# Feed-forward up products by seven half-size products, and modulation sums moved to other stages

## The reference

```python
def conv_glu(h, w_up, conv_w, conv_b, w_down):
    gate, val = jnp.split(h @ w_up, 2, axis=-1)          # h 256x1024, w_up 1024x5632
    gate = causal_dwconv(gate, conv_w) + conv_b          # 3 taps along the tokens
    return (jax.nn.silu(gate) * val) @ w_down            # w_down 2816x1024
...
for i in range(DEPTH):
    ...
    x = x + conv_glu(rms_norm(x, norm_ffn_w[i]), ffn_w_up[i], ffn_conv_w[i], ffn_conv_b[i], ffn_w_down[i])
...
cond = jax.nn.silu(c)
mod = cond @ w_ada[l] + b_ada[l]                         # w_ada 1024x6144, one row of condition
```

## Time and profile before

| | us |
|---|---|
| median of 3 runs | 2525.71 |
| lowest and highest run | 2521.23, 2529.0 |
| the profiled execution | 2521.13 |
| its span | 2519.2 |

### The profile page before, as it was taken

The page is one execution under the profiler, slowest core; times in us unless marked ns, Lnnn a source line. Parts: engine busy times, 40 slices in busy tenths (PEclk is TensorE's granted clock), DMA queues, the critical chain, the costliest instruction groups (busy, mean ns, idle before and its releaser), DMA issues.

```text
span 2519.2 us, 29772 instructions
## 1 busy us (share of the span) xinstructions
PE 2257.0 (90%) x12084; PEld 1458.6 (58%) x12084; DVE 927.0 (37%) x2253; ACT 555.2 (22%) x1232; POOL 57.9 (2%) x86
## 2 busy tenths in 40 slices
PE   8999999999999999999998887788799988777875
PEld 7888768855875787467764333333468743333332
DVE  4764437431143556243433222222324342222223
ACT  4321411001152210031622111111214421111111
POOL 0010000000100000002000000000002000000000
PEclk9999999999999999999999999998899989999998
DMA  7221236774721767735248999999733459999996
GB/s 274 101 76 68 103 131 250 264 285 160 209 105 67 264 230 266 267 128 167 101 176 341 427 427 427 428 428 427 283 142 118 160 245 427 427 428 428 427 427 269
DMA packets 141890, 653.57 MB, mean 259 GB/s; under 512 B 7386, under 2 KB 13834, under 8 KB 117040
## 3 DMA queue, kind: packets, MB, share of 16 engines
q1 hardware_dynamic: 138336, 642.19, 64.3%
q0 software_dynamic: 3408, 9.38, 1.6%
HBM read 648.40 MB, written 3.15 MB: 259 GB/s over the span
## 4 chain that ended last, share of the span: by engine, by line
PE 65%; DMA 24%; DVE 6%; ACT 3%; issue 1%; DVEq 0%; ACTq 0%
PE ps L106 63%; DMA wring<-in_w_up 11%; DMA AR<-in_w_up 5%; DMA wring<-in_w_gate 5%; PE ps L109 2%; DMA bias_rows<-AR 2%; ACT AR L115 1%; DVE AR L125 1%; DMA AR<-in_w_gate 1%; DVE AR L129 1%; ACT L115 1%; DVE AR L120 1%; DVE AR L133 0%; DVE X L125 0%; DVE XN L133 0%
## 5 line engine op out<-in xcount | busy, mean ns | idle before, releaser
L106 PE MATMUL ps<-HT,wring 128*128 128x256 f32 x3200 | 720.5, 386 | 0.8 <-ACT wring L115 0.4
L106 PEld LDWEIGHTS ps<-HT,wring 128*128 128x128 f32 x3200 | 616.0, 194 | 92.5 <-issue 4.2
L106 PE MATMUL ps<-wring,AR 128*32 128x512 f32 (+3 forms) x1440 | 348.7, 597 | 22.4 <-DVE AR L125 21.1
L115 ACT ACTIVATE AR<-ps 128x512 f32<-128x512 f32 (+4 forms) x338 | 162.3, 480 | 900.0 <-PE ps L106 849.9
L106 PE MATMUL ps<-wring,MN 128*32 128x512 f32 (+1 forms) x1568 | 246.2, 649 | 91.1 <-DMA wring<-in_w_up 73.5
L106 PEld LDWEIGHTS ps<-wring,AR 128*32 128x32 f32 (+1 forms) x1440 | 133.9, 145 | 183.7 <-issue 178.9
L106 PEld LDWEIGHTS ps<-wring,MN 128*32 128x32 f32 (+1 forms) x1568 | 68.6, 122 | 257.7 <-DMA wring<-in_w_up 107.8
L141 DVE COPY AR<-ps 128x512 f32<-128x512 f32 (+4 forms) x99 | 58.8, 594 | 383.4 <-PE ps L106 380.9
L106 PE MATMUL ps<-AR 128*128 128x128 f32 (+5 forms) x1336 | 183.2, 380 | 10.5 <-DVE AR L125 8.1
L125 DVE TENSOR_TENSOR AR<-ps,AR 128x128 f32<-128x128 f32 (+3 forms) x148 | 63.1, 426 | 326.7 <-ACT AR L115 163.3
L106 PEld LDWEIGHTS ps<-AR 128*128 128x128 f32 (+3 forms) x1336 | 132.6, 173 | 41.2 <-issue 30.3
(11 more groups left out here) (152 smaller groups left out, 1667.6 us busy)
## 6 DMA issues: line engine op xcount, KB each, us to landing
wring<-in_w_up SPq DMA_DIRECT2D x46, 2048.0 KB, 31.0
wring<-in_w_down SPq DMA_DIRECT2D x46, 2048.0 KB, 31.7
wring<-in_w_gate SPq DMA_DIRECT2D x44, 2048.0 KB, 27.3
wring<-in_w_ada SPq DMA_DIRECT2D x24, 2048.0 KB, 12.8
wring<-in_ffn_w_up SPq DMA_DIRECT2D x20, 2048.0 KB, 8.3
AR<-in_w_gate SPq DMA_DIRECT2D x20, 2048.0 KB, 27.8
wring<-in_w_in SPq DMA_DIRECT2D x18, 2048.0 KB, 7.7
AR<-in_w_down SPq DMA_DIRECT2D x18, 2048.0 KB, 32.2
```

The lines of the kernel that those rows point to most:

```text
L106: return Ins(self.eng and self.eng.matmul(out, lhs, rhs, start=start, stop=stop), None)
L115: return Ins(self.eng and self.eng.activation(out, in_, func, **kw), self)
```

## The change

The product of a chunk's weights (two k-halves by two column halves, quarters a11, a12, a21, a22) with HT (two k-halves by two token halves, quarters b11 to b22) is made by Strassen's scheme in Winograd's form: seven products of quarters, each of four k-tiles against 128 tokens, instead of eight. VectorE forms four sums of token quarters once per layer (in XN, `TS`), and four sums of weight quarters per chunk: s1 into `SUMS`, s3, s2 and s4 in place in the weights. The products go in pairs to PA banks (p26, p57, p34) and the first to PB, from which ScalarE copies it (`KEPT`). VectorE combines them in `RAWS`, from where the taps and the multiplication read; the middle tap moves to ScalarE. The order of products on TensorE is 1, 2, 7, 5, 6, 3, 4; in the first two chunks products 1 and 2 come before the rest, those of chunk 0 even before token half 1 is turned. `up_sums` of chunks 0 and 1 stand on VectorE ahead of the output projection's additions.

The down loads now start with the one that needs value chunk 0, each group waits for its own value chunk, and a bank of PA is taken at its first use. The 24 modulations leave the up phase: eight go to `down` of each layer (one, two, two and three after the first four groups), eight to sparse attention (two after each of the first three chunks, one after each of the last two). SyncE's order of loads, TensorE's sums and VectorE's passes follow.

The core of the diff (lines left out are "..."):

```diff
+    SUMS = Ring([at(4096 + 1024 * j, 1024) for j in range(2)])
+    KEPT = Ring([at(6144 + 256 * j, 256) for j in range(2)])
+    RAWS = Ring([at(8752 - 1024 * j, 1024) for j in range(2)])
...
+    UPS = [(val, chunk) for val in range(2) for chunk in range(6)]
+    ADA_DOWN = [(0,), (1, 2), (3, 4), (5, 6, 7)]
+    ADA_NSA = [(8, 9), (10, 11), (12, 13), (14,), (15,)]
+    DOWNS = (1, 0, 2, 3, 4, 5)
...
+    def up_blocks(i):
+        return 2 if UPS[i][1] < 5 else 1
...
+        n = 128 * up_blocks(i)
+        wt = blocks(W[up_name(layer, i)], 8, 2 * n)
+        total = SUMS[up_name(layer, i)][:, 0:4 * n].rearrange("p (k n) -> p k n", k=4)
+        return wt[:, 0:4, 0:n], wt[:, 4:8, 0:n], wt[:, 0:4, n:2 * n], wt[:, 4:8, n:2 * n], total
...
-            for val in range(2):
-                for chunk in range(6):
-                    n = 512 if chunk < 5 else 256
-                    c0 = val * 2816 + chunk * 512
-                    weights(("up", layer, val, chunk), up[:, c0:c0 + n], 8, n)
-                    if chunk < 5:
-                        ada(12 * layer + 5 * val + chunk)
-            weights(("down", layer, 0), dn[2560:2816], 2, 1024)
-            ada(12 * layer + 10)
-            weights(("down", layer, 1), dn[0:512], 4, 1024)
-            ada(12 * layer + 11)
-            for c in range(1, 5):
-                weights(("down", layer, 1 + c), dn[c * 512:c * 512 + 512], 4, 1024)
+            for i, (val, chunk) in enumerate(UPS):
+                n = 256 * up_blocks(i)
+                c0 = val * 2816 + chunk * 512
+                weights(up_name(layer, i), up[:, c0:c0 + n], 8, n)
+            for g, j in enumerate(DOWNS):
+                c0, n = (512 * (j - 1), 4) if j else (2560, 2)
+                weights(("down", layer, j), dn[c0:c0 + 128 * n], n, 1024)
+                for a in ADA_DOWN[g] if g < 4 else ():
+                    ada(16 * layer + a)
...
+            for n in ADA_NSA[ch]:
+                ada(n)
...
-            for m in range(2):
-                for c in range(2):
-                    bank(e, PA, (tag, m, c))
...
+                        if n == 0:
+                            bank(e, PA, (tag, m, c))
...
+            def product(i, part):
+                name, nb = up_name(layer, i), up_blocks(i)
+                a11, a12, a21, a22, total = up_tiles(layer, i)
+                if part == 1:
+                    bank(e, PB, ("p1", name))
+                    place(name)
+                    lhs, rhs, to = a11, HT[:, 0:4, tok(0)], (PB["p1", name], 0)
+                    e.wait_ge(sig("norm_ha"), (tag, 0, 3))
+                elif part == 2:
+                    bank(e, PA, ("p26", name))
+                    lhs, rhs, to = a12, HT[:, 4:8, tok(0)], (PA["p26", name], 0)
+                    e.wait_ge(sig("norm_ha"), (tag, 0, 7))
+                elif part == 7:
+                    bank(e, PA, ("p57", name))
+                    lhs, rhs, to = a21, TS[2], (PA["p57", name], nb)
+                    e.wait_ge(vect, ("t", layer, 2))
+                    e.wait_ge(vect, ("s3", name))
+                elif part == 5:
+                    lhs, rhs, to = total, TS[0], (PA["p57", name], 0)
+                    e.wait_ge(vect, ("t", layer, 0))
+                    e.wait_ge(vect, ("s1", name))
+                elif part == 6:
+                    lhs, rhs, to = a11, TS[1], (PA["p26", name], nb)
+                    e.wait_ge(vect, ("t", layer, 1))
+                    e.wait_ge(vect, ("s2", name))
+                elif part == 3:
+                    bank(e, PA, ("p34", name))
+                    lhs, rhs, to = a12, HT[:, 4:8, tok(1)], (PA["p34", name], 0)
+                    e.wait_ge(sig("norm_ha"), (tag, 1, 7))
+                    e.wait_ge(vect, ("s4", name))
+                else:
+                    lhs, rhs, to = a22, TS[3], (PA["p34", name], nb)
+                    e.wait_ge(vect, ("t", layer, 3))
+                ps, b0 = to
+                for b in range(nb):
+                    for k in range(4):
+                        c = 128 * (b0 + b)
+                        ins = e.matmul(ps[:, c:c + 128], lhs[:, k, 128 * b:128 * b + 128], rhs[:, k, :], k == 0, k == 3)
+                ins.then_inc(done, (name, part))
+                if part == 4:
+                    W.free(name, (done, (name, 4)))
+                elif part == 5:
+                    SUMS.free(name, (done, (name, 5)))
+            product(0, 1)
+            product(0, 2)
             norm_half(tag, 1)
-            for val in range(2):
-                for chunk in range(6):
-                    n = 512 if chunk < 5 else 256
-                    name = ("up", layer, val, chunk)
-                    features(done, name, weights(name, 8, n), 8, HT, range(0, n, 128), tag)
-                    W.free(name, (done, (name, n // 256 - 1)))
-                    k = 12 * layer + 5 * val + chunk
-                    if chunk < 5 and k > 12 * layer:
-                        ada_sum(k - 1)
-            e.wait_ge(sig("ffn_v"), ("val", layer, 21))
-            srcs = [(("down", layer, 0), 20, 2)] + [(("down", layer, 1 + c), 4 * c, 4) for c in range(5)]
-            down(done, tag, srcs, G, [lambda n=n: ada_sum(12 * layer + 9 + n) for n in range(3)], None if layer else "nsa")
+            for i, part in ((1, 1), (1, 2), (0, 7), (0, 5), (0, 6), (0, 3), (0, 4), (1, 7), (1, 5), (1, 6)):
+                product(i, part)
+            PA.defer()
+            product(1, 3)
+            product(1, 4)
+            for i in range(2, 12):
+                for part in (1, 2, 7, 5, 6, 3, 4):
+                    product(i, part)
+            srcs = [(("down", layer, j), 4 * (j - 1) if j else 20, 4 if j else 2) for j in DOWNS]
+            ready = [(vect, ("val", layer, j - 1 if j else 5)) for j in DOWNS]
+            down(done, tag, srcs, G, [lambda ns=ns: [ada_sum(16 * layer + n) for n in ns] for ns in ADA_DOWN],
+                 None if layer else "nsa", ready)
...
+                for n in ADA_NSA[ch]:
+                    ada_sum(n)
...
+                for n in ADA_NSA[3 + ch]:
+                    ada_sum(n)
...
+            for i in range(2):
+                up_sums(layer, i)
...
+            a11, a12, a21, a22, total = up_tiles(layer, i)
+            v.wait_ge(slots[W.where[name]], name)
+            v.tensor_tensor(total, a21, a22, ADD).then_inc(done, ("s1", name))
+            v.tensor_tensor(a21, a11, a21, SUB).then_inc(done, ("s3", name))
...
+                v.wait_ge(mm, (name, part))
+                if part == 1:
+                    v.tensor_tensor(a11, total, a11, SUB).then_inc(done, ("s2", name))
+                else:
+                    v.tensor_tensor(a12, a12, a11, SUB).then_inc(done, ("s4", name))
...
+                v.wait_ge(act, ("p1", name))
+                v.wait_ge(mm, (name, 6))
+                v.tensor_tensor(r[:, :, :, 0, :], both(i, "p26"), two(p1), ADD).then_inc(done, ("u2", name))
+                KEPT.free(name, (done, ("u2", name)))
+                PA.free(("p26", name), (done, ("u2", name)))
+                v.tensor_tensor(r[:, :, :, 1, :], both(i, "p57"), two(r[:, 1, :, 0, :]), ADD).then_inc(done, ("u4", name))
...
+                v.wait_ge(mm, (name, 4))
+                v.tensor_tensor(crossed, both(i, "p34"), r[:, :, :, 1, :], ADD).then_inc(done, ("c21", name))
+                PA.free(("p34", name), (done, ("c21", name)))
+                v.tensor_tensor(r[:, 1, :, 1, :], both(i, "p57")[:, 0], r[:, 1, :, 1, :], ADD).then_inc(done, ("c22", name))
+                PA.free(("p57", name), (done, ("c22", name)))
...
+                if val:
+                    g = G[:, 4 * chunk:4 * chunk + n, :]
+                    v.wait_ge(act, ("gate", layer, 4 * chunk + n - 1))
+                    v.tensor_tensor(g, RAWS[name][:, 0:256 * n].rearrange("p (b t) -> p b t", b=n), g, MUL).then_inc(done, ("val", layer, chunk))
+                    RAWS.free(name, (done, ("val", layer, chunk)))
+                else:
+                    for b in range(n):
+                        f = 4 * chunk + b
+                        y, x = G[:, f, :], RAWS[name][:, 256 * b:256 * b + 256]
+                        v.wait_ge(act, ("center", layer, f))
+                        for d in (2, 1):
+                            ins = v.scalar_tensor_tensor(y[:, d:256], x[:, 0:256 - d], vec("fconv", 66 * layer + f + 22 * (2 - d)), y[:, d:256], MUL, ADD)
+                            ins.then_inc(done, ("gate", layer, f) if d == 1 else None)
+                    RAWS.free(name, (done, ("gate", layer, f)))
...
+            b11, b12, b21, b22 = (HT[:, 4 * k:4 * k + 4, tok(m)] for k in range(2) for m in range(2))
+            v.wait_ge(sig("norm_mm"), (tag, 1, 1))
+            v.wait_ge(sig("norm_ha"), (tag, 0, 7))
+            v.tensor_tensor(TS[0], b12, b11, SUB).then_inc(done, ("t", layer, 0))
+            v.wait_ge(sig("norm_ha"), (tag, 1, 7))
+            v.tensor_tensor(TS[2], b22, b12, SUB).then_inc(done, ("t", layer, 2))
```

(54 more changed lines are left out.)

71 lines of the change are left out of this document (42 added, 29 removed).

## The result

The kernel after takes **2562.61 us** (median of 4 runs, 2559.54 to 2564.69), the kernel before 2525.99 (4 runs of the same chip): ratio **1.0146**, 95% interval 1.0127 to 1.0165. The forecast had the sign and most of the mechanisms, and was 17.6 us too low; the upper end of its range was missed by 0.6 us.

What follows compares the result with a forecast made beforehand. TensorE, busy 90% of the span, was taken as the bound. Gains of -39.1 and costs of +58.9 gave +19.8 us on the profiled 2521.1, so 2540.9; with 4.6 for the median, 2545 us, range 2517 to 2562.

Steps and rivals of the forecast that it cites:

- A: Up phase, TensorE: seven products of 128 columns for eight in 256-column calls, 303.6 us becomes 275.0, -28.6 us.
- B: Start of both up phases: products 1 and 2 of chunk 0 fill TensorE's gaps, -6.5 us, and one clock drop goes, -1.7.
- C: Passage from up to down: the first down group wants only value chunk 0, so the wait goes, -2.3 us.
- D: VectorE in the up phase: late sum in chunk 5, +4.8 us; satisfied waits and nearly full VectorE, +5 (0 to 17).
- E: Moved modulations in the downs: third sum after group 3 waits for its VectorE pass, +4.2 and +5.9 us (0 to 15).
- F: Moved modulations in sparse attention: loads held up by the bias-row write, then VectorE late, +35 us (13 to 45).
- the landing of `n2` at T+48: Sparse attention: third projection chunk's weights land 48 us after the first projection (T, 604.46 us); TensorE stalls 15 us.
- by T+24.5 about half of n2 has come: Sparse attention, when the bias-row write's slow part begins: 275 packets of that weight load still lie on held engines.
- Clock drops after the new stalls, 1.7 each: Sparse attention: two or three drops of TensorE's clock behind the new stalls, +4 us.
- 1: Rival, sparse attention: weight packets are not held up, one PSUM bank is; 12.6 us instead of 35, 2521 us, chance 0.15.
- 3: Rival, up phase: the seven products are not cheap, 0.1 to 0.2 us lost at each of 168; 2560 to 2575, chance 0.05.
- 2: Rival, sparse attention: the bias-row write no longer reaches into the projections, nothing there waits; 2507 us, chance 0.10.

## Why the prediction was right, and where it was short

- **A** right. In after the records keep 0.112 us, and the product stage is worth what the sum said, within 3 us (experiment with the products of before).
- **B, C** right: both gaps at the start and the one at the passage are gone.
- **D** right for chunk 5 (2.79 us for 2.4, and 6.7 us back when mended). The allowance for satisfied waits stands: A, B and D together came out 3 us worse, not better. That the up stages are still 6 us better than the -29.3 of A to D comes from the 10 us that the kernel with the old products has too: 2.3 are C, and about 5 are the clock, since before ran 17.1 us of its two up stages at the lower level and that kernel 6.8; the 10.2 that went are the three stretches behind narrow sums, which left this phase. The forecast had put nothing for that. The rest, some 3, has no cause shown.
- **E** had the size of the third sum's waits (4.90 and 6.03 for 4.2 and 5.9). Its cause was right in the first down; in the second it was luck, since 4.58 stay without the addition in the way, behind passes whose load came late. It was short by the **second** sum of the pair after group 2 (1.73 and 2.44 us), which the forecast didn't look at; there too passes stand behind a late load. In all 15.1 for 10.1.
- **F**, the largest term, came out nearly right, with one step wrong in it. The mechanism was right: write, then `n2`, then VectorE behind `in_w_ada` (38.00 us idle), hidden product at T+128.6 for T+121.6. **The step of F that failed is the landing of `n2` at T+48**, and in it "by T+24.5 about half of n2 has come". Modulation 11 stood ahead of `n2` in the same queue. Here is what the weights' queue had moved from 605 to 616.3 us (T+24.5), and then both queues from 634 to 650:

```profile
q1 hardware_dynamic: 1394, 2.82, 69.8%
...
q0 software_dynamic: 192, 0.79, 44.3%
q1 hardware_dynamic: 192, 0.39, 6.3%
```

 Some 1030 of the 1394 packets are modulation 11's, so about a third of `n2` had come, and most of that on the free engines: eight of the sixteen engines reported its landing by 620.4 us, the other eight between 652.4 and 654.3. The queues then went one for one, 12 packets a us each, as the forecast had it. Counted back from the landing at that rate, some 445 of the 512 packets on the held engines were still to come at T+24.5, where the forecast had 275 (an estimate). They came with the last of the write, T+62.5, and TensorE waited 28.38 us for 15. That the write is the cause is shown by its removal (-32).
 This error hardly moved the time, though. Behind `n2` the forecast let TensorE wait again from T+62 to T+82 for modulations 12 and 13, and that wait shrank to 6.67 us, since they landed nearly as forecast (T+68.6 and T+78.2 for T+67 and T+75). The two waits are 35.05 us, and F's +35 stands; that the late `n2` was paid for by the next wait is luck.
- **The clock is the step that made the number wrong.** The forecast had "Clock drops after the new stalls, 1.7 each", +4 in F, and put them at nothing in the downs and behind the hidden product. The rows show 16.76 for 14.00 and 23.71 for 20.87 us in the first down, 15.55 and 9.44 for 14.06 and 7.07 in attention, 6.23 for 3.70 at its end, and clock 0.96 for 1.00 with 5.4 us more in the stage behind it. Beyond the waits stand 9.6 us in the downs (24.7 less 15.1), 6.4 in attention (41.5 less 35.05) and 5.4 behind the hidden product: 21.4 for 4. At the lower level after ran 94 us of these four stages, before 6. Filling the waits gave 10.7 us back; the rest isn't divided by any run.
- **Sum.** Against -29.3, +10.1 and +39 (F with its clock) stand -35.2, +24.7 and +41.5, and +5.4 behind: 36.4 for 19.8, and 36.6 between the medians. The missing 17 are 5 of waits in the downs and 17.4 of what is put to the clock (9.6 in the downs, 2.4 in attention, 5.4 behind it), less 6 in up.
- **Rivals.** 1 and 3 are out (`n2` did wait; the records are cheap). 2 was right in that the slow write is what costs, but without it the loads don't fit either: -32 and not down to 2507.

 The Trainium skill ("DMA: Bandwidth & Descriptors", section "Queues, rings and completion order") has an engine take turns between queues by packets of typically 9 to 17 descriptors, by which, as the prediction read it, `n2` would have been in by T+30. The landing at T+62.5, and 192 packets to 192, speak against that reading. Its section "Rules for kernel authors" confines a transfer whose outermost dimension is smaller than 16 to at most that many engines; the trace agrees (eight rows, and q0 filled 44.3% of the 16 engines from 634 to 650 us), and spreading the rows took the write from 46.5 to 12.8 us, behind 5.4 for the one copy.

## What to carry to other kernels

Work that is moved out of a full stage takes its loads and its accumulator bank with it: before moving it, add up the bytes of the new stage against what the DMA engines have left there, and look for one slow transfer on few engines that everything behind it in the same queue will wait for. A wait of TensorE can cost its length and then some microseconds of slow clock behind it (15.1 us of waits in the two downs came with 9.6 more), and here narrow products had such stretches behind them with no wait at all; price a stage with both. Where an engine runs through a list of passes and additions, let the addition lag by the depth of the burst that follows, look at every place of the burst, not at the last only, and check at each whether the addition or the load comes last.

## What the runs showed of the hardware

- TensorE stood still for 28.38 us and had granted clock 0.50 for 30.7 us, 3 of them after work had begun again. A first down with waits of 1.7 and 4.9 us had 20.5 us at the lower level (clock 0.90); with these waits filled by dummy products it had 6.8 in one trace and none in another (0.97 and 1.00, 97.8 us for 103.4).
- In before the clock went to 0.50 for 3.4 us three times while TensorE never waited, each time 0.1 to 1.4 us behind 16 one-column records (2.08 us); behind a fourth such sum it stayed at 1.00.
- An issue of a 2 MB load, mostly 0.37 us on SyncE, took 32.27 us while earlier loads were held up; nothing waited behind it here but further loads.
- A write from 8 partitions to DRAM (2 MB, 46.5 us) held a load of 2 MB, asked in the same moment, for 46.5 us: eight of the sixteen engines had their part of the load in by 620.4 us, the other eight went packet for packet with the write (192 to 192 in 16 us). Written as 16 KB and copied from DRAM the same rows took 5.4 and 12.8 us.
- The second block, with the same instructions, took 1434.6 to 1442.8 us in 14 traces: a difference of half a per cent in one stage of a single trace need not come from that stage.
